# Moving the output normalisation of the first two head pairs to earlier stages of the second group, in a fused two-block kernel

## The reference

```python
S = S * w[:, :, None, :] + sa[..., None] * b[:, :, None, :] + v[..., None] * k[:, :, None, :]
y = jnp.einsum('bhij,bhj->bhi', S, r)          # for each of 512 tokens, eight heads
...
mu_y = jnp.mean(y, axis=-1, keepdims=True)
var_y = jnp.mean(jnp.square(y - mu_y), axis=-1, keepdims=True)
y = ((y - mu_y) * lax.rsqrt(var_y + GN_EPS)).reshape(B, S, MIX_B)
y = y * lnx_g.astype(f32) + lnx_b.astype(f32)
bonus = jnp.sum(rh * kh * r_k.astype(f32), axis=-1, keepdims=True) * vh
y = y + bonus.reshape(B, S, MIX_B)
return (y * g.astype(f32)).astype(p.dtype)
```

## Time and profile before

| | us |
|---|---|
| median of 3 runs | 1488.13 |
| lowest, highest | 1479.65, 1488.69 |
| the profiled execution | 1484.96 |
| its span, first to last instruction | 1483.1 |
| PE busy | 1392.3 (94%) |
| DVE busy | 648.0 (44%) |
| ACT busy | 560.2 (38%) |
| POOL busy | 495.9 (33%) |

### The profile page before, as it was taken

How to read it: one execution, slowest core, us unless ns; L and a number is a source line. 1 busy time by engine, 2 the same in 40 slices (tenths; PEclk the granted TensorE clock), 3 DMA queues, 4 the chain that set the end, 5 groups by cost and what they waited for, 6 DMA issues and landing times.

```text
span 1483.1 us, 22792 instructions
## 1 busy us (share of the span) xinstructions
PE 1392.3 (94%) x9482; PEld 1146.5 (77%) x9482; DVE 648.0 (44%) x1160; ACT 560.2 (38%) x836; POOL 495.9 (33%) x139
## 2 busy tenths in 40 slices
PE   4899999889899999999997999999999999998998
PEld 1687866775788888878887778888788888887886
DVE  2655677363555333330027524687345444452001
ACT  2435455243432322221214444555454343433122
POOL 1333233014333443433432231112233344443434
PEclk9899999998999999999998998999999999999999
DMA  9662265001312223233212620101221323222221
GB/s 355 188 152 82 86 229 201 31 3 58 113 58 103 96 85 114 85 108 117 88 60 69 249 81 5 58 30 58 72 86 57 114 85 108 92 88 97 96 75 57
DMA packets 24741, 147.93 MB, mean 100 GB/s; under 512 B 2716, under 2 KB 3868, under 8 KB 9024
## 3 DMA queue, kind: packets, MB, share of 16 engines
q1 hardware_dynamic: 19296, 130.96, 24.1%
q10 hardware_dynamic: 5344, 15.51, 3.9%
HBM read 141.74 MB, written 4.72 MB: 99 GB/s over the span
## 4 chain that ended last, share of the span: by engine, by line
PE 82%; DVE 9%; ACT 3%; issue 2%; DMA 2%; POOL 2%; SPq 0%; ACTq 0%; DVEq 0%; POOLq 0%
PE bank L2009 23%; PE bank L2011 22%; PE bank L2010 22%; PE bank L2268 5%; PE bank L1161 2%; DMA raw<-in_weights 2%; POOL weight_lo L1272 2%; PE bank L2175 1%; PE bank L1152 1%; ACT weight_hi L1317 1%; PE bank L1143 1%; DVE bank L1656 1%; PE bank L1070 1%; DVE xres L1656 1%; PE bank L1139 1%
## 5 line engine op out<-in xcount | busy, mean ns | idle before, releaser
L1272 POOL TENSOR_TENSOR weight_lo<-raw,weight_hi 128x2048 fp32r<-128x2048 f32 x98 | 445.7, 4548 | 838.1 <-ACT weight_hi L1317 838.0
L2009 PE MATMUL bank<-act_hi,weight_hi 128*128 128x512 f32 (+1 forms) x1136 | 436.5, 384 | 22.4 <-DVE act_lo L1653 7.1
L2011 PE MATMUL bank<-act_hi,weight_lo 128*128 128x512 f32 (+1 forms) x1136 | 427.3, 376 | 0.0
L2010 PE MATMUL bank<-act_lo,weight_hi 128*128 128x512 f32 (+1 forms) x1136 | 427.1, 376 | 0.0
L1317 ACT ACTIVATE weight_hi<-raw 128x2048 fp32r<-128x2048 f32 x98 | 185.2, 1891 | 403.1 <-PE bank L2011 394.4
L2009 PEld LDWEIGHTS bank<-act_hi,weight_hi 128*128 128x128 f32 x1136 | 218.2, 192 | 63.0 <-issue 15.8
L2011 PEld LDWEIGHTS bank<-act_hi,weight_lo 128*128 128x128 f32 x1136 | 217.7, 192 | 38.9
L2010 PEld LDWEIGHTS bank<-act_lo,weight_hi 128*128 128x128 f32 x1136 | 218.2, 192 | 35.0 <-issue 0.2
L2009 PE MATMUL bank<-weight_hi,hid_hi 128*128 128x512 f32 x352 | 139.0, 395 | 6.9 <-DVE acc L1656 4.7
L2010 PE MATMUL bank<-weight_lo,hid_hi 128*128 128x512 f32 x352 | 138.8, 394 | 0.0
L2011 PE MATMUL bank<-weight_hi,hid_lo 128*128 128x512 f32 x352 | 138.4, 393 | 0.0
(11 more groups left out here) (361 smaller groups left out, 1720.7 us busy)
## 6 DMA issues: line engine op xcount, KB each, us to landing
raw<-in_weights SPq DMA_DIRECT2D x120, 1024.0 KB, 4.6
w<-in_w ACTq DMA_DIRECT2D x2, 2048.0 KB, 10.4
bias_rows<-grow ACTq DMA_DIRECT2D x1, 2560.0 KB
xres<-in_x SPq DMA_DIRECT2D x4, 512.0 KB, 6.7
strip<-bias_rows ACTq DMA_DIRECT2D x1, 2048.0 KB, 9.0
out<-xres SPq DMA_DIRECT2D x3, 512.0 KB, 2.6
row_a<-in_ln_g ACTq DMA_DIRECT2D x2, 512.0 KB, 3.9
row_b<-in_ln_b ACTq DMA_DIRECT2D x2, 512.0 KB, 4.8
```

Source lines behind the costliest of these rows:

```text
L1272: pool.tensor_tensor(wlo[i % SPLIT][:, :size], raw[n % RAW][:, :size], whi[i % SPLIT][:, :size], ALU.subtract).then_inc(lo_ready, 1)
L2009: pe.matmul(o, l[0], r[0], start=first, stop=False)
L2010: pe.matmul(o, l[0], r[1], start=False, stop=False)
L2011: return pe.matmul(o, l[1], r[0], start=False, stop=last)
```

## The change

The seven entries of `AT_END` get other stages as keys. Before, the parts of the normalisation of pairs 0 and 1 stand behind the stages m(2) to g1(2); in the change, behind q4(3) to m2(2). Nothing else is edited, and no instruction is added or removed. In the table a key is (stage, pair within the group), so `("q4", 1)` is q4(3).

```diff
-AT_END = {("m", 0): [("norm", 0, 0), ("norm", 1, 0)], ("m", 1): [("norm", 0, 1), ("norm", 0, 2)],
-          ("m2", 0): [("norm", 1, 1), ("norm", 1, 2), ("norm", 0, 3), ("norm", 0, 4)],
-          ("m2", 1): [("norm", 1, 3), ("norm", 1, 4), ("norm", 0, 5)], ("z4", 0): [("norm", 0, 6), ("norm", 1, 5)],
-          ("z4", 1): [("norm", 1, 6), ("norm", 0, 7)], ("g1", 0): [("norm", 1, 7)]}
+AT_END = {("q4", 1): [("norm", 0, 0), ("norm", 1, 0)], ("r2", 0): [("norm", 0, 1), ("norm", 0, 2)],
+          ("r2", 1): [("norm", 1, 1), ("norm", 1, 2)], ("tb", 1): [("norm", 0, 3), ("norm", 0, 4)],
+          ("r3", 0): [("norm", 1, 3), ("norm", 1, 4), ("norm", 0, 5)], ("m", 0): [("norm", 0, 6), ("norm", 1, 5)],
+          ("m", 1): [("norm", 1, 6), ("norm", 0, 7)], ("m2", 0): [("norm", 1, 7)]}
```

## The result

| | before | the change |
|---|---|---|
| median | 1481.99 us (20 runs) | 1475.53 us (20 runs) |
| lowest, highest | 1472.63, 1488.81 | 1464.38, 1481.81 |
| the profiled execution | 1484.96 | 1473.71 |
| its span, mean granted clock | 1483.1, 0.970 | 1471.9, 0.976 |

The ratio is 0.9946 with a 95% interval of 0.9930 to 0.9963, so the change saves 8.0 us of 1482, with an interval of 5.5 to 10.4 (the medians lie 6.5 apart). It is faster and within 1%, as forecast; but the forecast counted on 4.7 us, which lies outside the interval. The mechanism was right, its size was not.

What follows compares the result with a forecast made beforehand. The prediction took PE, busy 94% of the span, as the bound. It summed 5.23 + 0.77 - (0.1 + 0.6 + 0.2 + 0.4) = 4.7 us of gain, giving 1481 us from several baselines (1480.3 from the profiled 1484.96); range 1475 to 1488.

Steps and rivals of the forecast that it cites:

- The wait and the slow clock, 5.23 us: Around z4(3): PE's 3.86 us wait ahead of the transposes goes, and 0.88 + 0.49 us of slow clock.
- DVE in time, and no slack: From r2 to m: DVE finishes the moved normalisation in time, with 0.1 us of new wait ahead of m(2).
- ACT: New PE waits for ACT's drains: 0.6 us ahead of z4(3), 0.2 ahead of g1(2), 0.4 ahead of g1(3).
- Part 0 moved "without a price": The state products of the output, moved from behind m(2) to behind q4(3), cost PE 1.48 us at either place.
- 0.45 ahead of m(3): PE's 0.45 us wait ahead of m(3), for a bank ACT drains, goes since m(3) gets other banks.
- The 0.32 us ahead of z4(2): PE's 0.32 us wait for ACT ahead of z4(2) goes, since the normalisation's squares leave ACT's queue there.
- The sum: Over the whole stretch: 5.23 + 0.77 - (0.1 + 0.6 + 0.2 + 0.4) = 4.7 us gained.
- the zero: Behind the edit, the slow-clock stretch from 345 to 356 us was counted as neither gain nor loss.
- the bound of 2 us: A shift of the slow-clock stretch from 345 to 356 us gains or loses at most 2 us.
- POOL blocking DVE: Pair 1's last DVE multiplication waits for POOL, PE's transposes wait 2.4 us; about 1483.5 us, chance 5%.
- the slower case: DVE holds m(2) some 1.5 us, the clock falls under m and m2; 6.3 us lost, 1486.5 us, chance 7%.
- No gain: Later PE work waits for a weight tile or POOL's low parts, or the clock falls; about 1485 us, chance 13%.

Runs made afterwards that it cites:

- x7_more: The change with DVE's mean reduction done three times instead of once for pairs 0 and 1; 1483.97 us, one execution.
- x6_burst: The change with all of DVE's normalisation work for pairs 0 and 1 in one lump ahead of r3; 1485.22 us, one execution.
- x3_split: The change with transposes and POOL's last part back at their old places behind z4(2) to g1(2); 1474.86 us, ratio 0.9944 to the kernel before.
- x5_part0: The kernel before with only the state products of the output and DVE's four sums moved early, behind q4(3); 1482.76 us, one execution.
- x1_before: The kernel before, unedited, traced a second time; 1485.12 us, one execution.
- x4_late_turn: The kernel before with only the transposes and POOL's last part moved later, the transposes behind g1(3) and g2(2); 1483.19 us, one execution.
- x2_after: The change, unedited, traced a second time; 1480.13 us, one execution.
- x9_after: The change, unedited, timed once more beside the kernel before; 1475.45 us (12 runs), ratio 0.9941.
- x8_port: The change with pair 1's last DVE normalisation step behind m(3), beside POOL's work for pair 0, and pair 1's later parts moved back; 1480.50 us, one execution.
- the split order: The change with transposes and POOL's last part at their old places, one kernel timed twice; 1474.86 us (ratio 0.9944) and 1476.11 us (0.9961).

## Why the prediction was right in kind and short in size

Each of its steps, from PE's starts in the two traces.

- **The wait and the slow clock, 5.23 us: right.** From z4(2) to g1(2) it was 326.07 - 317.58 = 8.49 us, and is 321.76 - 318.84 = 2.92. With the transposes at their new place, 0.59 + 0.58 us from start to start, that is 8.49 - 2.92 - 1.17 = 4.40 us gained; the prediction's terms for the same piece are 5.23 - 0.6 - 0.2 = 4.43.
- **DVE in time, and no slack: right.** 0.15 us ahead of m(2) for 0.1; x7_more and x6_burst show the edge on the other side.
- **ACT: right.** 0.59 for 0.6 ahead of z4(3); 0.2 for 0.2 ahead of g1(2), which the row doesn't show in brackets but the starts do (321.76 - 320.53 = 1.23, against 1.03 from z4(2) to the transposes behind it in x3_split); 0.20 for 0.4 ahead of g1(3).
- **Part 0 moved "without a price", and 0.45 ahead of m(3): the gain was too small.** The prediction took 1.48 us for part 0 at both places. From part 0 to m(3) it was 309.75 - 307.82 = 1.93 us. Early, between the drain of q4(3) and r2(2), it adds (299.98 - 298.39) - (297.03 - 296.47) = 1.03, since from its first start to its last modelled end it overlaps its neighbours. The gain is 0.90 us, not 0.45. x5_part0 has 0.8.
- **The 0.32 us ahead of z4(2): too small.** From m2(2) to z4(2) it was 317.58 - 313.31 = 4.27, and is 318.84 - 315.23 = 3.61: 0.66.
- **A gap in m(3) that the prediction put at nothing, 0.67 us.** Before, from m(3) to m2(2) it was 313.31 - 309.75 = 3.56; now 314.65 - 311.76 = 2.89. Before, the products of z stand here for 0.34 us, on PE's timeline of the first trace; x1_before has the same gap with 0.61, and no trace of the change has it, nor has x5_part0, where only part 0 moved; x4_late_turn, where part 0 stayed, has it with 0.34. (The last row is the start of g2.)

```profile
312.83 0.59 PE L2268 MATMUL bank<-z,dur 64*64 64x128 f32 x10 [0.34 <-issue]
313.31 1.09 PE L2268 MATMUL bank<-dur 64*64 64x64 f32 x30
...
328.04 0.28 PE L2268 MATMUL bank<-z,blk 64*64 64x64 f32 x8
```

On the other side m(2) itself is later by (308.28 - 299.98) - (305.09 - 297.03) = 0.24, and takes 311.17 - 308.28 = 2.89 for 307.82 - 305.09 = 2.73, 0.16 more. The sum to g1(2) is 4.40 + 0.90 + 0.66 + 0.67 - 0.24 - 0.16 = 6.23 us, which is all of A; g1 takes 323.97 - 321.76 = 2.21 for 328.04 - 326.07 = 1.97, so that it is 6.0 at g2. **The step that failed is "The sum": its 0.77 for the small waits that go, against 1.3 for those that come.** Those that go measure 0.90 + 0.66 + 0.67 = 2.23 us, those that come 0.24 + 0.16 + 0.83 (z4, 5.23 - 4.40) + 0.24 = 1.47. So they are worth +0.8 us together, not -0.5, and 5.23 + 0.8 is the 6.0 at g2. Three terms carry the miss: part 0 at 1.48 us where it costs 1.03, the gap in m(3) at nothing, and z4(2)'s wait taken at the number in brackets. That number counts from a matmul's modelled end, and without a wait the next stage starts before that end: z4(2) now starts at 318.84 where the row before it, 318.02 + 1.04, ends at 319.06. So a wait of 0.32 us takes 0.54 from start to start. The remaining 0.1 us of the 0.66, and what the gap in m(3) is, stay open.

What ACT's conversion, the next consumer, has of the 6.0 is 39.41 and 39.53 us from the drain in the two traces of before against 33.16, 34.03 and 33.75 in the three of the change: on average 5.8.

**The rest is the clock.** B is 59.86 and 59.98 before and 51.31, 56.04 and 54.19 in the change, on average 6.1 less, with 4.7 us of spread among traces of one kernel; the prediction took what follows the edit at zero and allowed 2 us either way. Against the 6.5 us that A gains on average, the three traces have 2.1 more, 2.6 less and 0.7 less at B: the zero was about right, and the bound of 2 us a little narrow for a single trace. Further on, a stretch near 890 us is at 1.2 GHz for 17.1 us in the first trace of before and for 3.4 in the first trace of the change, as the windows of both show; but x1_before, x2_after and x9_after all have 17.1 there. Behind B the two first traces differ by (1483.1 - 1471.9) - (356.33 - 349.70) = 4.6 us more, and the other traces give no reason to put that down to the change.

```profile
882.00:902.00 20.00, 18.92 (x73) 16.31 (x74) 9.06 (x34) 5.49 (x16) 4.37 (x1) 0.57 0.14 52
```

```profile
874.00:894.00 20.00, 17.54 (x104) 15.61 (x104) 10.36 (x38) 7.37 (x18) 4.53 (x1) 0.91 0.16 53
```

The timed runs say it more evenly. Within 20 runs of the change the time falls by 1.10 us for each 0.001 of mean clock, within the 23 of before timed beside x9_after by 1.03 (straight lines through the listed times and clocks). At a clock of 0.975 these lines stand at 1473.9 us (20 runs) and 1474.7 (12 runs) for the change and at 1479.4 for before: 4.7 to 5.5 us that the clock doesn't explain, each line being good to some 0.3 to 0.6 us (one standard error). The mean clock is 0.9737 and 0.9753 against 0.9723, which is 1.5 to 3.3 us of time at 1.10 us for 0.001, and of these the 0.88 + 0.49 us behind the long wait are shown place by place. Whether the remaining 0.1 to 1.9 us are a lasting effect of the change (a PE that stands less further on) or the scatter of the clock isn't settled by these runs: a mean clock of so many runs is itself only good to about 0.001.

**The forecast time.** 1481 us rested on a profiled run of 1484.96 and a median of 1488.13 over three runs; over 20 runs before is at 1482. The mean of the four times shown, 1485.4, lies 3.4 us above that; the rest of the 5.5 us by which the forecast is above the median of the change is the size of the gain and a rounding.

**The rivals.** POOL blocking DVE (5%) did not occur, by 0.63 us (312.80 against 313.43), and cost 0.24 us, not the 2.4 given, in the one order where the two met (x8_port). Of the slower case (7%) the wait and the clock are real, at 1.86 and 1.96 us of waiting in x6_burst and x7_more, and the change stays clear of it with 0.15. They cost 4.0 us of A there, not 6.3: the stretch at 1.2 GHz behind the wait was 3.4 us long, not 10. A stays 2.2 us and more below before, so an order slower than the kernel before was not shown. Nor does 1.5 us of waiting decide: the same 1.57 us left the clock at 1.00 in x9_after (last section). "No gain" (13%) is refuted: 5.8 us arrive at the mixer, and the interval's lower end is 5.5 us of gain. What it named, PE waiting for POOL's low parts, does occur at out1 (0.75 us in the first trace), but POOL had come forward with the drain.

## What to carry to other kernels

Price a wait by the distance from start to start against a place where the same two stages follow each other without one; the idle number in the row was short by 0.07 to 0.22 us here (0.59 took 320.53 - 318.84 - 1.03 = 0.66, the 0.15 ahead of m(2) took 0.24, 0.32 took 0.54). Work that shares a queue with a stage's drains has to be moved with all its steps to where that queue has room, and spread there: moving only the instruction that waits (x4_late_turn), only its first step (x5_part0), or all of it in a lump (x6_burst) gave 1.0 to 3.2 us of A where the change gave 6.2 to 6.7, in one trace each. Where the clock varies by itself, compare distances up to a landmark close behind the edit, several traces of each, and let timed runs speak for the whole.

## What the runs showed of the hardware

- **The clock behind waits.** It was at 1.2 GHz (windows of 0.52 to 0.71 with their edges) behind waits of PE of 3.86 (all three traces that have it), 1.86, 1.96, and 2.25 with 0.88 us, and stayed at 1.00 behind those of 0.59, 0.54, 0.20 and 0.15 us. Behind 1.57 us it went both ways: in the kernel before it was 0.72 from 278 to 284 us, in x9_after, with the same wait at the same place, 1.00. PE's timeline and windows of x9_after:

```profile
277.72 0.52 PE L2420 MATMUL bank<-hs,gts 64*64 64x64 f32 x8 [1.57 <-DVE hs L1861]
```

```profile
278.00:284.00 6.00, 5.99 (x102) 4.09 (x102) 2.51 (x7) 1.47 (x3) 0.82 (x1) 1.00 0.02 3
```

Nor does a long wait have to stand ahead: behind yl the clock fell in every trace, in the first of before at about 343.5 us, with no wait over 0.63 us in the 7 us ahead of it.
- **The same kernel gets a different clock.** Behind yl, where PE's work is the same in all traces of the change, the stretch at 1.2 GHz was 3.4, 13.7 and 10.2 us long (first trace, x2_after, x9_after). B differs by up to 4.7 us between them, 0.9 of which arise before ACT's conversion (34.03 against 33.16), the rest behind it.
- **A gap that belongs to an instruction.** In g2 PE stands ahead of one and the same product in every trace but that of x4_late_turn, with nothing to wait for that the profile shows. On PE's timeline of the first trace of the change:

```profile
326.29 0.29 PE L2268 MATMUL bank<-z,blk 64*64 64x64 f32 x5 [0.72 <-issue]
```

It is 0.71 and 0.53 us in the two traces of before, 0.17 in x5_part0, 0.72, 1.45 and 1.20 in the change, 0.99 and 1.26 in the split order, 1.48 in x8_port, 1.52 in x6_burst, 1.81 in x7_more. It varies by 0.7 us between traces of one kernel and doesn't follow the waits ahead of it (x7_more has a long one and the longest gap), so it moves up to 0.9 us between the change and before. The gap in m(3) is put down to issue too. What either is was not tried.
